# RetNet and RG-LRU decoder layer on one core: the recurrent stage with another gelu, paired exponentials and woven gate tiles

## The chip, the cores and the metric

The kernel runs on one core of one Trainium2 chip. The metric is the device time in microseconds (us), the median of the runs. The core has a matrix engine (TensorE, PE in the profile, with PEld for its weight loads), a vector engine (VectorE, DVE), an activation engine (ScalarE, ACT), a third elementwise engine (GpSimd, POOL) and SyncE (SP), which here only issues transfers.

## The reference, cut to what matters

One decoder layer is computed for 512 prompt tokens and 8 sequences of 4 sample tokens, 544 columns in all, model width 1024. All products are fp32. The part that matters is the recurrent branch, 1536 channels in 12 blocks of 128:

```python
xr, gr = two column blocks of h @ w_in
xconv = causal_conv(xr, conv_buf, conv_w, conv_b)
r = sigmoid(xconv @ w_rg_a + b_rg_a); i = sigmoid(xconv @ w_rg_x + b_rg_x)   # 12 blocks of 128x128
log_a = -8 * r * softplus(-lru_param);  a = exp(log_a)
h_t = a_t * h_(t-1) + sqrt(-expm1(2 * log_a)) * (i * xconv)                  # over time
rnn_y = h * gelu(gr);  branch_rnn = rnn_y @ w_br_rnn
gb = sigmoid(h @ w_mgate + b)        # second half; multiplies branch_rnn
mod = silu(c) @ w_ada + b_ada        # six 1024-wide pieces, for 9 conditioning vectors
```

The retention branch, the mix, the output product and a gated feed-forward network follow.

## The kernel before, in words

Channels lie on the partitions and the 544 tokens on the free axis. A weight slab is 128 x 1024 numbers (512 KB; some are shorter). Each slab is loaded by SyncE, in the one order of the plan. ScalarE then writes its rounded high part (`w_hi`, L982) and VectorE the remainder (`w_lo`, L1276), into rings of three slots. TensorE computes hi*hi, hi*lo and lo*hi for each 128x128 block, each in two halves of 272 columns (`three_passes`, L644), so a tile with eight blocks is 48 matmuls. `split_to(s)` in each engine's program does the splits up to slab s, and `ahead(key)` does them up to two slabs beyond the tile's slab. The high part of slab s can't be written before slab s-3 is multiplied. A product tile lies in one of two PSUM places in turn and must be taken (`took`) before the next but one tile starts.

Every engine has a program written out by hand, and its order sets everything. In the recurrent stage the loop runs over n = 0 to 11. TensorE multiplies the xr tile n, then the small recurrent gates of tile n-1 (`recurrent_gates`, L744, eight fp32 matmuls), then the gr tile n. ScalarE takes xr out of PSUM (four pieces, L1084 to L1088), computes for tile n-1 the two sigmoids, a tanh, an exp and a square root (L1056 to L1062), does the next split, copies gr out of PSUM (L990), and gives the sigmoid of the gelu (L1097), once GpSimd has made its argument. GpSimd makes the gelu from the copy of gr with three products and a final one (L1740 to L1746), and multiplies the input gate with the convolution (`ii`, L1726). VectorE does the convolution (L1353, L1355), the decays (L1364 to L1368), the recurrence with a scan (L1373 to L1383) and the output and its hi and lo parts (L1386, L1284, L1285). `decays` and `recur` of tile n-1 stand at the end of iteration n.

Two loops over eight tiles follow: the gate tiles `gb` (h as the moving side), then the branch tiles `bn` (y as the moving side, 12 blocks in two slabs of 768 columns). Both carry the late part of the modulation: eight chunks of four slabs, each slab four matmuls of 512 columns with the conditioning vectors stationary (`modulation`, L690). One slab stands behind each half tile. Every second tile a finished chunk is copied out by ScalarE (`ada_row`, L1072), turned by TensorE (L700) and added by VectorE (`ada_out`, L1323 and L1324).

Of the kernel before, what the change touches and what calls it, by code (L numbers as in the profile page):

```python
# [24 lines left out]
ALU = mybir.AluOpType  # L25
# [4 lines left out]
P = 128  # L30
# [141 lines left out]
GB_PARTS = (KD // 2, KD // 2)  # L172
# [3 lines left out]
def later_slabs(name, m):  # L176

    first = START_SLABS + 2 * (m + (KD if name == "bn" else 0))
    return first, first + 1


def make_plan():
# [59 lines left out]
    for n in range(NR):  # L242
        pl.whole(("xr", n), 1, [KD])
        if n:
            pl.use_pair(("r", n - 1), 2)
            pl.use_pair(("i", n - 1), 3)
        pl.whole(("gr", n), 1, [KD])
    pl.use_pair(("r", NR - 1), 2)
    pl.use_pair(("i", NR - 1), 3)
    for name, parts in (("gb", GB_PARTS), ("bn", BN_PARTS)):  # L250
        for m in range(KD):
            pl.add_tile((name, m))
            for i, j in enumerate(later_slabs(name, m)):
                pl.add_slab((name, m, "w", i), parts[i] * P)
                pl.step((name, m, "w", i), (name, m))
                chunk_slab(j)
# [33 lines left out]
def slab_source(w, key):  # L290
# [6 lines left out]
    if kind == "gb":  # L297
        return w["w_gb"][key[1], :, key[3] * GB_PARTS[0] * P:(key[3] + 1) * GB_PARTS[0] * P]
# [16 lines left out]
def hybrid_layer_kernel(nc, w, out):  # L315
# [6 lines left out]
    with ExitStack() as top:  # L322
# [51 lines left out]
        gr = sb(rnn, "gr", [P, 2, T])  # L374
        gelu_t = sb(rnn, "gelu_t", [P, T])
        gelu = sb(rnn, "gelu", [P, 2, T])
        rr = sb(rnn, "rr", [P, T])
# [92 lines left out]
        gelu_arg, gelu_sig, gelu_ready, ix_ready = (sem(n) for n in ("gelu_arg", "gelu_sig", "gelu_ready", "ix_ready"))  # L470
# [160 lines left out]
        def _(pe):  # L631
# [115 lines left out]

            for n in range(NR):
# [5 lines left out]
            def turn_later(c):  # L754
                pe.wait_ge(*pair_freed(("ad", c)))
                dst, full = take_pair(("adt", c))
                ada_turn(ada_row[:, c % 2, :], dst[:, 0, :], full)

            recurrent_gates(NR - 1)
            def project_with_modulation(name, m, parts, hi, lo):  # L760


                c = ADA_START + (m + (KD if name == "bn" else 0)) // 2 - 1
                project((name, m), parts, hi, lo, after=[lambda q=q: modulation(q) for q in later_slabs(name, m)],
                        before_last=(lambda: turn_later(c)) if m % 2 == 0 and c >= ADA_START else None)

            for m in range(KD):
                project_with_modulation("gb", m, GB_PARTS, h_hi, h_lo)
            pe.wait_ge(y_ready, NR)
            for m in range(KD):  # L770
                project_with_modulation("bn", m, BN_PARTS, y_hi, y_lo)
# [195 lines left out]
        def _(act):  # L967
# [79 lines left out]
            def gates(n):  # L1047
# [6 lines left out]
                i, u, e, root = (t[:, n % 2, :] for t in (ii, uu, ee, su))  # L1054
                wait_pair(act, ("r", n))
                do(A(halves(rr[:]), ps[:, 4:6, 0:HALF], ACT.Sigmoid, bias=vcol("b_a", n)), *pair_freed(("r", n)))  # L1056
# [3 lines left out]
                do(A(u, rr[:], ACT.Tanh, scale=c4[:, n:n + 1]), u_ready)  # L1060
# [3 lines left out]
            def modulation_rows(name, m):  # L1064

                c, i = divmod(later_slabs(name, m)[1], ADA_PARTS)
                split_to(pl.slab[("ad", c, "w", i)] + AHEAD)
                if i == ADA_PARTS - 1:
                    act.wait_ge(multiplied, pl.tile_end[("ad", c)])
                    if c >= ADA_START + 2:  # L1070
                        wait_pair(act, ("adt", c - 2))
                    do(A(ada_row[:, c % 2, :], ps[0:2 * NSEQ, 4, :], ACT.Copy), *pair_freed(("ad", c)), wait=False)  # L1072

            act.wait_ge(h_ready, KD)
            for n in range(NR):
# [14 lines left out]
                if n:  # L1090
                    gates(n - 1)
                ahead(("gr", n))
                if n >= 2:
                    act.wait_ge(gelu_ready, n - 1)
# [3 lines left out]
            for m in range(KD):  # L1098
                ahead(("gb", m))
                if m == 0:  # L1100
                    gates(NR - 1)
                split_to(pl.slab[("gb", m, "w", 1)] + AHEAD)

                evacuate(("gb", m), gbr[:, m, :], ACT.Sigmoid, bias=vcol("b_gb", m))
                modulation_rows("gb", m)
            for m in range(KD):
                split_to(pl.slab[("bn", m, "w", 1)] + AHEAD)
                modulation_rows("bn", m)
# [155 lines left out]
        def _(dve):  # L1264
# [105 lines left out]
            def recur(n):  # L1370
# [13 lines left out]
                dve.wait_ge(gelu_ready, n + 1)  # L1384

                do(V.tensor_tensor(bb[:], hs[:], gelu[:, n % 2, :], ALU.mult))  # L1386
# [6 lines left out]
            for n in range(NR):  # L1393
# [3 lines left out]
                if n:  # L1397
                    decays(n - 1)
# [518 lines left out]
```

## Time and profile before

| | us |
|---|---|
| median of 3 runs | 1546.73 (1546.11 to 1549.68) |
| span of the profiled execution, first to last instruction | 1542.5 |
| PE busy | 1422.0 (92%) |
| DVE busy | 859.4 (56%) |
| ACT busy | 568.5 (37%) |
| POOL busy | 281.9 (18%) |

The profile gives no other time of its own for the execution than its span; it is 4.2 us under the median of the runs. A busy PE is not PE at its peak, and an engine's share is an average over stages that have different limits, so the stage that the change touches is read by itself.

### The profile page before, as it was taken

To read this page: it belongs to the slowest core of one execution; us is meant where nothing else is said; L and a number is where in the kernel's file an instruction comes from. 1 tells how busy PE (TensorE), PEld (TensorE's weight loads), DVE (VectorE), ACT (ScalarE), POOL (GpSimd) and SP (SyncE) were. 2 spreads that over 40 slices of the span, in tenths; PEclk is the share of its full clock that TensorE was granted. 3 is DMA by queue.
4 is the path that set the end of the run, shared out by engine and by line. 5 is a ranking of instruction groups with operands and counts; after the bars stand their busy time and mean duration, and the time that the engine had idled before them with its cause. 6 is when DMAs were issued, how large, how long until landed. Compare 5 with 4: busy or idle time off the path is not lost.

```text
span 1542.5 us, 24001 instructions
## 1 busy us (share of the span) xinstructions
PE 1422.0 (92%) x10168; PEld 1311.7 (85%) x10168; DVE 859.4 (56%) x1022; ACT 568.5 (37%) x769; POOL 281.9 (18%) x352
## 2 busy tenths in 40 slices
PE   5798887899999999999999999999499999999994
PEld 2498777789999788889879988999399999999993
DVE  4699999844436367537635854773743333332224
ACT  5477666543333332323133232434332222212220
POOL 3364555100012313311320231000200000000002
PEclk9799998999999999999999999999699999999997
DMA  7122112465442524432541443223022222232321
GB/s 319 69 70 68 56 58 86 132 208 169 163 158 94 177 89 148 155 117 85 176 163 62 147 154 123 79 95 145 0 83 92 87 86 93 82 91 76 88 76 58
DMA packets 49499, 172.70 MB, mean 112 GB/s; under 512 B 5488, under 2 KB 5616, under 8 KB 49008
## 3 DMA queue, kind: packets, MB, share of 16 engines
q1 hardware_dynamic: 39024, 135.51, 26.9%
q0 software_dynamic: 9216, 33.56, 6.5%
q10 hardware_dynamic: 1152, 2.10, 0.4%
q8 instruction: 80, 1.31, 0.4%
q14 instruction: 27, 0.22, 0.0%
HBM read 149.82 MB, written 21.32 MB: 111 GB/s over the span
## 4 chain that ended last, share of the span: by engine, by line
PE 64%; DVE 6%; ACT 1%; issue 1%; ACTq 0%; DVEq 0%
PE ps L644 54%; PE ps L853 2%; PE ps L864 2%; PE ps L836 1%; PE ps L880 1%; PE ps L890 1%; PE ps L882 1%; DVE mo L1645 1%; DVE x_res L1646 1%; PE ps L711 1%; DVE s_lo L1458 0%; PE ps L793 0%; DVE rsn L1641 0%; PE ps L806 0%; DVE work L1523 0%
## 5 line engine op out<-in xcount | busy, mean ns | idle before, releaser
L644 PE MATMUL ps<-h_hi,w_hi 128*128 128x272 f32 x2240 | 475.8, 294 | 40.6 <-DVE w_lo L1276 22.3
L644 PE MATMUL ps<-h_hi,w_lo 128*128 128x272 f32 x2240 | 467.6, 291 | 0.0
L644 PE MATMUL ps<-h_lo,w_hi 128*128 128x272 f32 x2240 | 466.2, 290 | 0.0
L644 PEld LDWEIGHTS ps<-h_hi,w_hi 128*128 128x128 f32 x2240 | 359.2, 191 | 51.8 <-issue 39.6
L1276 DVE TENSOR_TENSOR w_lo<-raw,w_hi 128x1024 fp32r<-128x1024 f32 (+3 forms) x204 | 246.4, 1208 | 233.2 <-ACT w_hi L982 229.9
L644 PEld LDWEIGHTS ps<-h_lo,w_hi 128*128 128x128 f32 x2240 | 356.6, 191 | 0.0
L644 PEld LDWEIGHTS ps<-h_hi,w_lo 128*128 128x128 f32 x2240 | 354.0, 191 | 0.0
L982 ACT ACTIVATE w_hi<-raw 128x1024 fp32r<-128x1024 f32 (+3 forms) x204 | 203.0, 995 | 219.8 <-PE ps L644 178.1
L1811 POOL TENSOR_TENSOR mo<-mo,rsn 128x512 f32<-128x512 f32 x6 | 9.6, 1597 | 566.6 <-DVE rsn L1641 566.6
L1558 DVE SCALAR_TENSOR_TENSOR state<-state,ps 128x512 f32<-128x512 f32 x64 | 41.1, 684 | 111.3 <-PE ps L890 111.2
L644 PE MATMUL ps<-a_hi,w_hi 128*128 128x272 f32 x352 | 73.6, 291 | 2.1 <-DVE a_lo L1285 2.1
L644 PE MATMUL ps<-a_hi,w_lo 128*128 128x272 f32 x352 | 73.3, 290 | 0.0
L644 PE MATMUL ps<-a_lo,w_hi 128*128 128x272 f32 x352 | 73.2, 290 | 0.0
L1276 DVE TENSOR_TENSOR w_lo<-ada_late,w_hi 128x1024 fp32r<-128x1024 f32 x32 | 40.2, 1257 | 51.0 <-ACT w_hi L982 50.5
L1145 ACT ACTIVATE s_hi<-state 128x1024 fp32r<-128x1024 f32 x32 | 33.9, 1060 | 81.9 <-PE ps L882 81.9
L1755 POOL DMA_DIRECT2D state<-in_state x32 | 23.4, 731 | 219.5 <-PE ps L700 130.7
L644 PEld LDWEIGHTS ps<-a_hi,w_hi 128*128 128x128 f32 x352 | 56.0, 190 | 2.3 <-DVE a_lo L1285 2.3
L982 ACT ACTIVATE w_hi<-ada_late 128x1024 fp32r<-128x1024 f32 x32 | 33.8, 1057 | 65.3 <-PE ps L644 65.3
L644 PEld LDWEIGHTS ps<-a_lo,w_hi 128*128 128x128 f32 x352 | 56.0, 191 | 0.0
L644 PEld LDWEIGHTS ps<-a_hi,w_lo 128*128 128x128 f32 x352 | 55.5, 191 | 0.0
L690 PE MATMUL ps<-w_hi,c_st 128*18 128x512 f32 x96 | 40.5, 422 | 15.6 <-DVE w_lo L1276 15.5
L644 PE MATMUL ps<-r_hi,w_hi 128*128 128x272 f32 x256 | 53.2, 289 | 1.8 <-DVE acc L1509 1.1
(228 smaller groups left out, 2010.5 us busy)
## 6 DMA issues: line engine op xcount, KB each, us to landing
raw<-in_w_head SPq DMA_DIRECT2D x48, 512.0 KB, 3.6
raw<-in_w_fin SPq DMA_DIRECT2D x44, 512.0 KB, 3.5
ada_late<-in_w_ada SPq DMA_DIRECT2D x32, 512.0 KB, 4.2
state<-in_state POOLq DMA_DIRECT2D x32, 512.0 KB, 4.2
out_rs<-state POOLq DMA_DIRECT2D x32, 512.0 KB, 3.5
raw<-in_w_rnn SPq DMA_DIRECT2D x24, 512.0 KB, 3.7
ada_raw<-in_w_ada SPq DMA_DIRECT2D x16, 512.0 KB, 14.4
raw<-in_w_bret SPq DMA_DIRECT2D x16, 512.0 KB, 3.5
```

What stands on the lines that cost most here:

```text
L644: mm = nc.tensor.matmul(dst[:, half, :], a, b[:, half * HALF:(half + 1) * HALF], start=first and j == 0, stop=last and j == 2)
L690: mm = nc.tensor.matmul(dst[0:2 * NSEQ, :], c_st[:, 2 * i + j, :], part[:, s % RING, j * ADA_CHUNK:(j + 1) * ADA_CHUNK], start=i == 0 and ...
L711: mm = nc.tensor.matmul(ps[:, pl.bank[key][0], 0:HALF], ccol("ones"), src[:, half * HALF:(half + 1) * HALF], start=k == 0, stop=k == n - 1)
L836: mm = nc.tensor.matmul(dst[:, 0:SEQ - j * P], k_r[:, d, j * P:(j + 1) * P], q_r[:, d, j * P:SEQ], start=d == 0, stop=d == 1)
L853: mm = nc.tensor.matmul(dst[:, j * P:SEQ], v_tok[:, j, o * P:(o + 1) * P], scores(j), start=j == 0, stop=j == JT - 1, skip_group_check=True)
L864: mm = nc.tensor.matmul(dst[:, :], k_tok[:, j, d * P:(d + 1) * P], v_tok[:, j, :], start=j == 0, stop=j == JT - 1)
L880: nc.tensor.matmul(ps[0:2 * NS, 7, :], q_st[:, d, at:at + 2 * NS], s_hi[:, e], start=b == 0 and d == 0, stop=False, skip_group_check=True)
L982: A(w_hi[:, i % RING, 0:cols], src[:, 0:cols], ACT.Copy).then_inc(hi_ready, 1)
L1145: do(A(s_hi[:, :], state[:, u % STATES, :, :].rearrange("p d e -> p (d e)"), ACT.Copy), s_hi_ready, wait=False)
L1276: V.tensor_tensor(w_lo[:, i % RING, 0:cols], raw_slab(i)[0][:, 0:cols], w_hi[:, i % RING, 0:cols].bitcast(F32), ALU.subtract).then_inc(lo_ ...
L1558: do(V.scalar_tensor_tensor(state[:, u % STATES, d, :], state[:, u % STATES, d, :], gamma(h) ** TS, ps[:, pl.bank[key][0], :], ALU.mult, A ...
L1755: pool.dma_start(state[:, u % STATES, :, :], w["state"][b, h].rearrange("(d p) e -> p d e", p=P))\
```

## The change

The gelu is one ScalarE instruction with its own function (`Gelu_apprx_tanh`), read straight from PSUM. GpSimd keeps only `ii` and the small copies. Exponentials and roots are no longer made tile by tile: at even n they are made for tiles n-2 and n-1, two exponentials and then two roots (`roots_at`). VectorE's decays and recurrence are done one iteration later, for tile n-2 (`recurrences_at`); iteration 11 does tiles 9 and 10, and tile 11 comes after the first split of the last gate tiles. Gate tiles 0 to 3 are multiplied in iterations 1, 4, 7 and 10, and tiles 4 to 7 in iteration 11 (`GATE_TILES`), each with one slab in place of two half slabs. The modulation is carried by the branch tiles alone: two slabs behind each half tile, so that a branch tile carries a whole chunk.

```diff
-GB_PARTS = (KD // 2, KD // 2)
+GATE_TILES = {1: (0,), 4: (1,), 7: (2,), 10: (3,), NR - 1: (4, 5, 6, 7)}
-def later_slabs(name, m):
+def later_slabs(m, part):
-    first = START_SLABS + 2 * (m + (KD if name == "bn" else 0))
+    first = ADA_PARTS * (ADA_START + m) + 2 * part
     return first, first + 1
+def roots_at(n):
+    if n == NR - 1 or n == NR:
+        return (n - 1,)
+    return (n - 2, n - 1) if n and n % 2 == 0 else ()
+def recurrences_at(n):
+    if n == NR - 1:
+        return (n - 2, n - 1)
+    return (n - 1,) if n == NR else (n - 2,) if n >= 2 else ()
...
# TensorE
                 project(("gr", n), [KD], h_hi, h_lo)
+                if n == NR - 1:
+                    recurrent_gates(n)
+                for m in GATE_TILES.get(n, ()):
+                    project(("gb", m), [KD], h_hi, h_lo)
             for m in range(KD):
+                def modulate(part, m=m):
+                    for q in later_slabs(m, part):
+                        modulation(q)
+                c = ADA_START + m - 1
+                project(("bn", m), BN_PARTS, y_hi, y_lo, y_ready if m == 0 else None, 0,
+                        after=[lambda: modulate(0), lambda: modulate(1)],
+                        before_last=(lambda c=c: turn_later(c)) if m else None)
...
# ScalarE: gates(n) keeps two sigmoids and the tanh
-                do(A(e, rr[:], ACT.Exp, scale=c2n[:, n:n + 1]), e_ready, wait=False)
-                do(A(root, u, ACT.Sqrt), su_ready, wait=False)
+            def roots(tiles):
+                for n in tiles:
+                    do(A(ee[:, n % 2, :], rr[:, n % 2, :], ACT.Exp, scale=c2n[:, n:n + 1]), e_ready, wait=False)
+                for n in tiles:
+                    do(A(su[:, n % 2, :], uu[:, n % 2, :], ACT.Sqrt), su_ready, wait=False)
...
                 if n:
                     gates(n - 1)
+                roots(roots_at(n))
                 ahead(("gr", n))
-                evacuate(("gr", n), gr[:, n % 2, :])
-                act.wait_ge(gelu_arg, n + 1)
-                do(A(gelu_t[:], gelu_t[:], ACT.Sigmoid, scale=GELU_C), gelu_sig, wait=False)
+                if n >= 3:
+                    act.wait_ge(y_ready, n - 2)
+                wait_tile(act, ("gr", n))
+                do(A(halves(gelu[:, n % 3, :]), out_tile(("gr", n)), ACT.Gelu_apprx_tanh), *took(("gr", n)), wait=False)
+                if n == NR - 1:
+                    gates(n)
+                    roots(roots_at(NR))
+                for m in GATE_TILES.get(n, ()):
+                    ahead(("gb", m))
+                    evacuate(("gb", m), gbr[:, m, :], ACT.Sigmoid, bias=vcol("b_gb", m))
...
# VectorE
                 ahead(("xr", n))
                 conv(n)
                 ahead(("gr", n))
-                if n:
-                    decays(n - 1)
-                    recur(n - 1)
+                for i in recurrences_at(n):
+                    decays(i)
+                    recur(i)
+                for m in GATE_TILES.get(n, ()):
+                    ahead(("gb", m))
+                    if n == NR - 1 and m == GATE_TILES[n][0]:
+                        for i in recurrences_at(NR):
+                            decays(i)
+                            recur(i)
             for m in range(KD):
+                split_to(pl.slab[("bn", m, "w", 1)] + AHEAD)
                 wait_took(dve, ("gb", m))
                 wait_tile(dve, ("bn", m))
...
-                if m % 2 == 0:
-                    ada_out(ADA_START + (KD + m) // 2 - 1)
+                if m:
+                    ada_out(ADA_START + m - 1)
...
# GpSimd: the four gelu instructions go
-                do(G.tensor_tensor(gelu_t[:], g, g, ALU.mult))
-                do(G.tensor_scalar(gelu_t[:], gelu_t[:], 0.044715, 1.0, ALU.mult, ALU.add))
-                do(G.tensor_tensor(gelu_t[:], gelu_t[:], g, ALU.mult), gelu_arg)
-                do(G.tensor_tensor(gelu[:, n % 2, :], g, gelu_t[:], ALU.mult), gelu_ready)
```

`rr` and `gelu` get two and three buffers for one and two; `gr` and `gelu_t` go.

## Rows read from the trace of the kernel before

**Rows 1.** Waits by engine: TensorE, 60 to 434 us; total us, times, longest.

```profile
PE ps L644 <- DVE w_lo L1276: 22.3, 13, 3.4
PE ps L744 <- DVE xc L1355: 7.4, 1, 7.4
PE ps L690 <- DVE w_lo L1276: 3.5, 2, 1.8
```

**Rows 2.** Windows: span; busy (instructions) of PE, PEld, DVE, ACT, POOL; clock, DMA.

```profile
78.60:432.40 353.80, 319.83 (x2268) 295.10 (x2268) 271.55 (x337) 201.90 (x268) 112.53 (x119) 0.97 0.34 111
...
184.00:201.50 17.50, 14.46 (x105) 13.57 (x105) 16.91 (x22) 11.60 (x18) 9.44 (x11) 1.00 0.19 61
```

**Rows 3.** Timeline, TensorE: start, us, instruction, idle before and its releaser.

```profile
84.70 2.00 PE L744 MATMUL ps<-xc,rg_w 128*128 128x272 f32 x8
86.33 0.61 PE L644 MATMUL ps<-h_hi,w_hi 128*128 128x272 f32 x2
...
194.90 0.49 PE L644 MATMUL ps<-h_hi,w_hi 128*128 128x272 f32 x2 [2.76 <-DVE w_lo L1276]
```

**Rows 4.** Chain that ended last, in order of time: one tile of eight blocks.

```profile
445.54 6.02 PE ps L644 x48
```

**Rows 5.** Timeline, VectorE, 185 to 201 us: one recurrence, then a convolution.

```profile
185.66 0.43 DVE L1364 TENSOR_SCALAR ee<-ee 128x544 f32<-128x544 f32 x1
...
190.19 1.29 DVE L1383 TENSOR_TENSOR_SCAN hs<-uu,bb 128x544 f32<-128x544 f32 x1
...
193.52 1.23 DVE L1276 TENSOR_TENSOR w_lo<-raw,w_hi 128x1024 fp32r<-128x1024 f32 x1
194.67 1.84 DVE L1353 SCALAR_TENSOR_TENSOR xc<-xp,vec,xc 128x512 f32<-128x512 f32 x1
...
200.03 0.75 DVE L1353 SCALAR_TENSOR_TENSOR xc<-xp,vec,xc 128x512 f32<-128x512 f32 x1
...
200.98 2.26 DVE L1276 TENSOR_TENSOR w_lo<-raw,w_hi 128x1024 fp32r<-128x1024 f32 x1
```

**Rows 6.** Groups by line and shape: GpSimd, 60 to 300 us; busy us, mean ns.

```profile
L1726 POOL TENSOR_TENSOR ii<-ii,xc 128x544 f32<-128x544 f32 x12 | 25.9, 2162 | 0.5 <-ACT uu L1060 0.5
```

**Rows 7.** Timeline, ScalarE, 200 to 210 us: one tile's gates, exponential and root.

```profile
201.49 0.79 ACT L1084 ACTIVATE xc<-ps,vec 128x544 f32<-128x544 f32 x1
...
202.79 0.73 ACT L1056 ACTIVATE rr<-ps,vec 128x544 f32<-128x544 f32 x1
...
206.22 0.75 ACT L1061 ACTIVATE ee<-rr,c2n 128x544 f32<-128x544 f32 x1
206.99 1.28 ACT L1062 ACT_TABLE_LOAD   x1
...
208.85 1.04 ACT L982 ACTIVATE w_hi<-raw 128x1024 fp32r<-128x1024 f32 x1
209.80 0.60 ACT L990 ACTIVATE gr<-ps 128x544 f32<-128x544 f32 x1
```

**Rows 8.** Timeline, a branch tile: TensorE, ScalarE and VectorE.

```profile
386.31 0.39 PE L690 MATMUL ps<-w_hi,c_st 128*18 128x512 f32 x1
...
387.23 0.41 PE L644 MATMUL ps<-y_hi,w_hi 128*128 128x272 f32 x2
...
391.73 0.40 PE L690 MATMUL ps<-w_hi,c_st 128*18 128x512 f32 x1
...
397.25 0.42 PE L700 MATMUL ps<-con,ada_row 18*128 18x18 f32 x4
...
386.57 1.06 ACT L982 ACTIVATE w_hi<-ada_late 128x1024 fp32r<-128x1024 f32 x1 [3.63 <-PE ps L644]
...
388.02 0.83 ACT L982 ACTIVATE w_hi<-raw 128x768 fp32r<-128x768 f32 x1
...
388.88 0.96 DVE L1276 TENSOR_TENSOR w_lo<-raw,w_hi 128x768 fp32r<-128x768 f32 x1
```

**Rows 9.** Transfers, 300 to 434 us: count, KB each, median us to landing.

```profile
ada_late<-in_w_ada SPq DMA_DIRECT2D x23, 512.0 KB, 4.2
```

More of the change, by code:

```diff
@@ L247, in make_plan @@
         pl.whole(("gr", n), 1, [KD])
+        for m in GATE_TILES.get(n, ()):
+            pl.whole(("gb", m), 1, [KD])
     pl.use_pair(("r", NR - 1), 2)
     pl.use_pair(("i", NR - 1), 3)
[L250 to L255, printed above, removed]
+    for m in range(KD):
+        pl.add_tile(("bn", m))
+        for i, n in enumerate(BN_PARTS):
+            pl.add_slab(("bn", m, "w", i), n * P)
+            pl.step(("bn", m, "w", i), ("bn", m))
+            for j in later_slabs(m, i):
                 chunk_slab(j)
@@ L297, in slab_source @@
     if kind == "gb":
[L298 removed]
+        return w["w_gb"][key[1]]
     if kind == "bn":
@@ L373, in hybrid_layer_kernel @@
         xc = sb(rnn, "xc", [P, 2, T])
[L374 to L377, printed above, removed]
+        gelu = sb(rnn, "gelu", [P, 3, T])
+        rr = sb(rnn, "rr", [P, 2, T])
         ii = sb(rnn, "ii", [P, 2, T])
@@ L1059, in gates, with modulation_rows @@
                    wait=False)
-                do(A(u, rr[:], ACT.Tanh, scale=c4[:, n:n + 1]), u_ready)
-                do(A(e, rr[:], ACT.Exp, scale=c2n[:, n:n + 1]), e_ready, wait=False)
-                do(A(root, u, ACT.Sqrt), su_ready, wait=False)
[L1064 to L1072, printed above, removed]
+                do(A(u, rr[:, n % 2, :], ACT.Tanh, scale=c4[:, n:n + 1]), u_ready)
+            def roots(tiles):
[3 more added lines that the diff above has]
+                    do(A(su[:, n % 2, :], uu[:, n % 2, :], ACT.Sqrt), su_ready, wait=False)
+            def modulation_rows(m):
+                c = ADA_START + m
+                split_to(pl.slab[("ad", c, "w", ADA_PARTS - 1)] + AHEAD)
+                act.wait_ge(multiplied, pl.tile_end[("ad", c)])
+                if m >= 2:
+                    wait_pair(act, ("adt", c - 2))
+                do(A(ada_row[:, c % 2, :], ps[0:2 * NSEQ, 4, :], ACT.Copy), *pair_freed(("ad", c)), wait=False)
             act.wait_ge(h_ready, KD)
@@ L1091, in _ @@
                     gates(n - 1)
+                roots(roots_at(n))
                 ahead(("gr", n))
-                if n >= 2:
-                    act.wait_ge(gelu_ready, n - 1)
-                evacuate(("gr", n), gr[:, n % 2, :])
-                act.wait_ge(gelu_arg, n + 1)
-                do(A(gelu_t[:], gelu_t[:], ACT.Sigmoid, scale=GELU_C), gelu_sig, wait=False)
[L1098 to L1105, printed above, removed]
+                if n >= 3:
[8 more added lines that the diff above has]
+                    evacuate(("gb", m), gbr[:, m, :], ACT.Sigmoid, bias=vcol("b_gb", m))
             for m in range(KD):
                 split_to(pl.slab[("bn", m, "w", 1)] + AHEAD)
-                modulation_rows("bn", m)
+                modulation_rows(m)
             def gn_squares(h):
@@ L1711, in _, with inputs, last @@
                 do(G.memset(xp[:, i, 0:3], 0.0))
+            def inputs(n):
+                pool.wait_ge(u_ready, n + 1)
+                do(G.tensor_tensor(ii[:, n % 2, :], ii[:, n % 2, :], xc[:, n % 2, :], ALU.mult), ix_ready, wait=False)
+            def last(n):
+                pool.wait_ge(scanned, n + 1)
+                do(G.tensor_copy(rnn_out[:, n, 0:1], hs[:, SEQ - 1:SEQ]), wait=False)
+                do(G.tensor_copy(rnn_out[:, n, 1:9], samples(hs)[:, :, TS - 1]), last_saved, wait=False)
             for n in range(NR):
```

70 lines of the change are left out of this document (18 added, 52 removed).

## The prediction

> **What bounds the kernel now.** I read the page first: TensorE is busy for 92% of the span and carries most of the chain that ended last, so time is won only where TensorE waits or runs at a low clock. Its busy digits are lowest in the first fifth, outside the load at the start. The list of TensorE's waits from 60 to 434 us [rows 1] shows who is late: VectorE, with the low part of the weights (22.3 + 3.5 us) and once with a convolution (7.4 us). The windows of one iteration [rows 2] show why: of 17.50 us VectorE is busy for 16.91, ScalarE for 11.60. The recurrent stage runs at VectorE's pace. The timeline of VectorE [rows 5] shows that part of this pace is not its own work. The six convolution instructions take 6.31 us (194.67 to 200.98), though the last pair takes 0.95 us, which would be 2.85 for three; a weight split takes 2.26 where another takes 1.23. The long ones lie beside GpSimd's products, and GpSimd is busy for 9.44 us of the tile [rows 2], most of it for the gelu.
>
> **What TensorE needs from 78.6 to 432.4 us**, first to last instruction of the stretch that the change touches. A tile of eight blocks takes 6.02 [rows 4], gates 1.63 (84.70 to 86.33) [rows 3], half a branch tile 4.50 and a modulation slab 0.92 [rows 8], a turn 0.42. So 22 xr and gr tiles 132.4, 12 gates 19.6, 8 gate tiles 48.2, 16 half branch tiles 72.0, 32 slabs 29.4, 8 turns 3.4: 305.0 us. The stretch takes 353.8 [rows 2], so 48.8 is lost: 33.2 in the listed waits [rows 1], about 10.6 to the clock (0.97 granted, 3% of 353.8), the rest in starts after waits. The change leaves TensorE's work as it is. It can give back at most these 48.8, and the question is which new waits stand in their place.
>
> **The change part by part.**
>
> *Gelu.* Four GpSimd instructions, a PSUM copy and a sigmoid of ScalarE become one ScalarE instruction. I price it as the PSUM copy, 0.60 [rows 7]. The trace does not show the function itself, nor whether it shares a table with the sigmoid. Bounds: no load or two loads of 1.28 a tile [rows 7]. I take two, since the exponential and the root each need one of their own here; I count 39 loads of the stage after and 37 now, so ScalarE is not relieved. The load before the gelu runs while ScalarE waits for gr, and it costs TensorE at most 0.3 us in iterations 4 and 10, where xr of the next tile needs gr's PSUM place.
> [...]
>
> *VectorE without the gelu beside it.* A recurrence takes 7.86 (185.66 to 193.52), 5.82 of it to the end of the scan; a split 1.15 start to start; a convolution 2.85 [rows 5]. With two splits that is 13.0 us a tile. What stays beside it is `ii` of 2.16 us [rows 6]. Bounds for what it costs VectorE: nothing, where it falls into idle time, or 2.2 a tile. VectorE lost 3.5 in a convolution and 1.0 in a split to about twice that much GpSimd work, so I take 1.1, in every second tile (in the other it falls where VectorE waits for ScalarE).
>
> *Pairs.* At even n the split of the next gr slab stands behind two exponentials and two roots, and VectorE's own split, and the recurrence behind it, wait for that. The loop is: scan of n-3 ends; ScalarE's gates, pair and split 8.4 (6.06 from 202.79 to 208.85, a second exponential 0.65 and root 0.56, split 1.04, hand-over) [rows 7]; VectorE split 1.15, recurrence 7.86, split 1.15, convolution 2.85, split 1.15, to the end of the next scan but one 5.82; with 1.1 beside GpSimd 29.5 us for two iterations. TensorE needs 27.3 for two iterations and 33.4 with a gate tile in them. So VectorE falls 2.2 behind in the two pairs without a gate tile and catches up in the others. Iteration 4, counted from the end of its xr tile: scan of tile 1 at 3.6, ScalarE to 12.0, VectorE's split 13.2, recurrence 21.0, low part of gr 5 at 22.2, while TensorE arrives at 1.63 + 3 x 6.02 + 1.63 = 21.3. So about 1.0 us is lost in each of iterations 4, 7 and 10, with the PSUM place 3.5 in all.
>
> *Iteration 11.* Counted from the end of xr 11: ScalarE takes it out in 1.3, then 6.06 and a split [rows 7], VectorE has the split of gate tile 5 at 9.6. Behind it stand two recurrences (15.7, with 1.1 beside GpSimd), then the split of gate tile 6, at 27.5. TensorE arrives at 1.63 + 6.02 + 1.63 + 12.04 = 21.3 and waits 6.2. Then the recurrence of tile 11 stands before the split of gate tile 7: 36.5, TensorE at 33.5, 3.0 more. The clock after such a wait: 1.6 us, an estimate, a sixth of the 10.6 lost now in six slow spells. The 7.4 us wait for the convolution goes: conv 11 is done 8 us before its gates.
>
> *Modulation behind the branch tiles.* Two slabs in place of one after each half tile. The ring of three then ties the next raw slab to the half tile just multiplied: ScalarE starts 0.26 after it, VectorE 0.86 later, 0.96 for the split, 0.14 to TensorE (194.75 to 194.90 in [rows 3, 5]): 2.22, against 1.84 of two modulation slabs [rows 8]. That is 0.38 lost in the middle of each of eight tiles, and about 0.25 at the end of seven, where VectorE also takes the tile and adds the turned chunk: 4.9 us. In exchange the half-width gate slabs go.
>
> *Buffers.* The third gelu buffer and the second `rr` are free of waits in this order. SyncE's list has the modulation slabs later and the gate slabs earlier, in the plan's order; at the start the slabs come as now.
>
> **The sum.** New losses 3.5 + 9.2 + 1.6 + 4.9 = 19.2, in place of 48.8: 29.6 less. The span goes from 1542.5 to 1512.9. The median of the runs lies 4.2 above the span now, so 1517 us.
>
> **The rivals.**
>
> (a) *TensorE never waits in the recurrent stage.* If VectorE runs ahead more than I work out, the 3.5 and most of the 9.2 go, and the time is 1505 (1498.6 were there no new wait at all). For it: the gate tiles bring 48 us of TensorE work with only 9 of VectorE's. Against: the three recurrences in a row in iteration 11 are in the program's order.
>
> (b) *The loop through both engines is longer.* If `ii` costs VectorE 2.3 in every tile and ScalarE's chain grows by 1 to 2 us, the loop is about 33 us a pair against 27.3 and 33.4: 5 lost in two pairs, 1 to 2 in three, 2 more at the end, 12 in all: 1529. For it: `ii` alone takes 2.16 now, and VectorE's own splits double beside GpSimd. [...]
>
> (c) *Slower: the branch tiles starve.* A branch tile brings four slabs of 512 KB and two of 384 KB in 13.1 us. The last modulation slab is asked for 3.9 us after the tile before ends, lands 4.2 later [rows 9] and is first needed 8.6 after it was asked for. To eat the whole gain each of eight tiles must lose 3.7 us, so the landing must take over 12.3 us. A landing of 14 us would lose 5.4 a tile, 43 in all, and give 1560. Against it: the transfers of the stretch are far from that.
>
> (d) *The change does nothing*, since something else sets the pace. TensorE's waits name VectorE each time, so this is hardly left.
>
> **How the numbers follow.** Forecast 0.68, (a) 0.12, (b) 0.14, (c) 0.04, (d) 0.02. The forecast's own range is 1510 to 1525 (each of 3.5, 9.2 and 4.9 from half to one and a half of itself). The range over the cases is 1506 to 1532. A change within 0.3% (4.6 us) can't be told from none in this kernel. Faster by more: 0.94; within: 0.03; slower: 0.03.
>
> **What would show it.** In the profile after: no `gelu_t`; splits of raw slabs near 1.23 and convolution pairs near 0.95 except beside `ii`; TensorE's waits for w_lo of some 6 and 3 us before gate tiles 6 and 7 and nowhere else above 1.5; the wait for xc gone; waits of 0.4 us before half the raw slabs of the branch tiles. The forecast is wrong if iterations 2 to 10 still take over 15 us without a gate tile, if the branch tiles take over 14.5 us each, or if the gelu instruction takes much more than 0.6.

## The result and the profile after

| | before | after |
|---|---|---|
| median of the four executions, us | 1548.02 | 1519.76 |
| median without the one at a low clock, us | 1548.02 | 1519.44 |
| span of the profiled execution, us | 1542.5 | 1517.3 |
| last turn of the late modulation, us from the start | 432.45 | 404.25 |

One of the four executions of the changed kernel ran at a granted clock of 0.556 throughout and took 2353.28 us; the ratio, 0.9815 with an interval of 0.9801 to 0.9829, and every comparison below go by the other three, 1519.44. The forecast was 1517.0, so it was 2.4 us too low (2.8 against the median of all four), and the gain is 28.6 us.

First the line of busy times of the changed kernel (busy us, share of the span, instructions).

```profile
PE 1421.0 (94%) x10168; PEld 1305.5 (86%) x10168; DVE 818.3 (54%) x1014; ACT 565.6 (37%) x751; POOL 221.8 (15%) x304
```

TensorE's work is the same (1421.0 us busy, 1422.0 before). GpSimd lost 60 us of work, and VectorE lost 41 us with only eight instructions fewer (1014 against 1022, half slabs joined).

TensorE's waits from 60 to 440 us, which answer to [rows 1]: total us, times, longest.

```profile
PE ps L658 <- DVE w_lo L1293: 11.0, 5, 5.9
```

The 13 waits for `w_lo` of [rows 1] are five, the two before modulation slabs are gone, and so is the one for `xc`. The timeline of TensorE shows where the five are, with two turns (L714) and the last one. The first of the five, 3.42 us, ends where the stretch begins; before has 2.92 us there, ended by ScalarE.

```profile
77.83 0.79 PE L658 MATMUL ps<-h_hi,w_hi 128*128 128x272 f32 x2 [3.42 <-DVE w_lo L1293]
...
156.24 0.49 PE L658 MATMUL ps<-h_hi,w_hi 128*128 128x272 f32 x2 [0.22 <-DVE w_lo L1293]
...
278.13 0.79 PE L658 MATMUL ps<-h_hi,w_hi 128*128 128x272 f32 x2 [5.94 <-DVE w_lo L1293]
...
287.13 0.49 PE L658 MATMUL ps<-h_hi,w_hi 128*128 128x272 f32 x2 [1.16 <-DVE w_lo L1293]
...
306.70 0.49 PE L658 MATMUL ps<-y_hi,w_hi 128*128 128x272 f32 x2 [0.23 <-DVE w_lo L1293]
...
318.16 0.42 PE L714 MATMUL ps<-con,ada_row 18*128 18x18 f32 x4
...
331.99 0.42 PE L714 MATMUL ps<-con,ada_row 18*128 18x18 f32 x4
...
404.25 0.42 PE L714 MATMUL ps<-con,ada_row 18*128 18x18 f32 x4 [0.76 <-ACT ada_row L1091]
```

The recurrent gates (L758) start 13.87 us after the last ones, or 19.88 where a gate tile is woven in, but for three iterations that take 0.14 to 0.45 more; before it was mostly 17.5 [rows 2]. The turns (L714) stand 13.83 apart, one for each branch tile. From the start after the first wait to the last turn it is 326.4 us, against 353.8 [rows 2].

The windows of the stretch and of two iterations, with the columns of [rows 2]:

```profile
77.80:404.30 326.50, 317.10 (x2269) 289.35 (x2269) 230.39 (x329) 199.17 (x250) 50.42 (x71) 0.98 0.37 121
...
202.20:230.20 28.00, 28.00 (x210) 27.06 (x209) 23.99 (x36) 21.07 (x29) 7.39 (x9) 1.00 0.28 92
```

In the second row TensorE is busy for all 28.00 us: the recurrent stage now runs at TensorE's pace. VectorE still has 4 us of room in it.

The groups by line and shape, 60 to 412 us (busy us, mean ns, idle before):

```profile
L1293 DVE TENSOR_TENSOR w_lo<-raw,w_hi 128x1024 fp32r<-128x1024 f32 x32 | 39.1, 1230 | 36.8 <-ACT w_hi L996 36.1
...
L1370 DVE SCALAR_TENSOR_TENSOR xc<-xp,vec,xc 128x512 f32<-128x512 f32 x36 | 34.7, 964 | 9.1 <-ACT xs L1107 8.3
L1372 DVE SCALAR_TENSOR_TENSOR xc<-xs,vec,xc 128x32 f32<-128x32 f32 x36 | 12.2, 338 | 0.0
...
L1726 POOL TENSOR_TENSOR ii<-ii,xc 128x544 f32<-128x544 f32 x12 | 21.6, 1802 | 6.0 <-ACT uu L1075 5.7
...
L1116 ACT ACT_TABLE_LOAD x12 | 15.4, 1283 | 5.8 <-PE ps L658 5.6
...
L1116 ACT ACTIVATE gelu<-ps 128x544 f32<-128x544 f32 x12 | 7.5, 625 | 0.7 <-PE ps L658 0.6
```

The same view of before, 60 to 440 us:

```profile
L1353 DVE SCALAR_TENSOR_TENSOR xc<-xp,vec,xc 128x512 f32<-128x512 f32 x36 | 44.1, 1225 | 1.1 <-POOL xs L1716 0.2
L1276 DVE TENSOR_TENSOR w_lo<-raw,w_hi 128x1024 fp32r<-128x1024 f32 x25 | 39.8, 1592 | 16.5 <-ACT w_hi L982 15.8
L1355 DVE SCALAR_TENSOR_TENSOR xc<-xs,vec,xc 128x32 f32<-128x32 f32 x36 | 29.6, 821 | 0.0
```

`ii` took 2162 ns [rows 6]. So the same instructions became shorter on both engines: a split by 0.36 us, a wide convolution instruction by 0.26, a narrow one by 0.48, `ii` by 0.36. The gelu takes 0.625 us and one table load per tile; with the loads of the other functions there are 39 in the stage, as counted ahead.

### The profile page after: what moved, and what is told of

Read it like the earlier page. It is cut to its first block, busy times and chain, and to the rows that moved or that the text cites. A ratio compares the mean times of both kernels' runs of the same rounds, so it can differ in the third digit from the quotient of the medians.

```text
span 1517.3 us, 23874 instructions
## 1 busy us (share of the span) xinstructions
PE 1421.0 (94%) x10168; PEld 1305.5 (86%) x10168; DVE 818.3 (54%) x1014; ACT 565.6 (37%) x751; POOL 221.8 (15%) x304
## 4 chain that ended last, share of the span: by engine, by line
PE 65%; DVE 6%; ACT 1%; issue 1%; ACTq 0%; DVEq 0%
PE ps L658 55%; PE ps L867 2%; PE ps L878 2%; PE ps L850 1%; PE ps L894 1%; PE ps L904 1%; PE ps L896 1%; DVE mo L1655 1%; DVE x_res L1656 1%; DVE s_lo L1468 0%; PE ps L725 0%; PE ps L807 0%; DVE rsn L1651 0%; PE ps L820 0%; DVE work L1533 0%
## 5 line engine op out<-in xcount | busy, mean ns | idle before, releaser
L1293 DVE TENSOR_TENSOR w_lo<-raw,w_hi 128x1024 fp32r<-128x1024 f32 (+2 forms) x196 | 236.2, 1207 | 277.6 <-ACT w_hi L996 274.0
L996 ACT ACTIVATE w_hi<-raw 128x1024 fp32r<-128x1024 f32 (+2 forms) x196 | 202.0, 1031 | 284.4 <-PE ps L658 229.3
L1683 DVE TENSOR_TENSOR a_tmp<-a_tmp,ps 128x544 f32<-128x544 f32 x22 | 15.9, 721 | 70.3 <-PE ps L658 70.3
L658 PE MATMUL ps<-r_lo,w_hi 128*128 128x272 f32 x256 | 52.9, 288 | 0.0
L658 PE MATMUL ps<-r_hi,w_lo 128*128 128x272 f32 x256 | 52.8, 287 | 0.0
```

The lines of the kernel that those rows point to most:

```text
L658: mm = nc.tensor.matmul(dst[:, half, :], a, b[:, half * HALF:(half + 1) * HALF], start=first and j == 0, stop=last and j == 2)
L996: A(w_hi[:, i % RING, 0:cols], src[:, 0:cols], ACT.Copy).then_inc(hi_ready, 1)
L1293: V.tensor_tensor(w_lo[:, i % RING, 0:cols], raw_slab(i)[0][:, 0:cols], w_hi[:, i % RING, 0:cols].bitcast(F32), ALU.subtract).then_inc(lo_ ...
L1683: do(V.tensor_tensor(halves(t), halves(t), out_tile(("fu", n)), ALU.mult), *took(("fu", n)))
```

## The experiments

Each was timed beside the kernel before, whose median was 1547.66 to 1547.96 in these sessions, within 0.4 us of the 1548.02 above. "The whole change" is the changed kernel with its 1519.44. The first four ask which part of the change carries the time.

**The gelu alone.** The kernel before, with the gelu in ScalarE and two `rr` buffers; order, pairs and modulation as before.

```diff
                 if n >= 2:
-                    act.wait_ge(gelu_ready, n - 1)
-                evacuate(("gr", n), gr[:, n % 2, :])
-                act.wait_ge(gelu_arg, n + 1)
-                do(A(gelu_t[:], gelu_t[:], ACT.Sigmoid, scale=GELU_C), gelu_sig, wait=False)
+                    act.wait_ge(y_ready, n - 1)
+                wait_tile(act, ("gr", n))
+                do(A(halves(gelu[:, n % 2, :]), out_tile(("gr", n)), ACT.Gelu_apprx_tanh), *took(("gr", n)), wait=False)
...
# GpSimd: its four gelu instructions go
```

> The kernel before with one part of the change: the gelu by one ScalarE instruction from PSUM, GpSimd's four gelu instructions gone (rr gets a second buffer so that nothing races). No pairs, no woven gate tiles, modulation as before. Theory G (the gelu beside VectorE and the wait of ScalarE for it were the loss): VectorE needs 13.0 us a tile and 1.1 beside ii, 14.1, TensorE 13.9; so iterations 1 to 11 take 14.1 to 14.5 us instead of 17.5, the 7.4 us wait for the convolution goes, and the time is 1512 to 1520, about that of the whole change. Rival W (the woven gate tiles are what gives VectorE room): with two more table loads a tile in ScalarE's chain and no gate tiles between, iterations stay near 16 us and the time is 1530 or more.

Measured: 1511.15 us (1509.85 to 1512.02), ratio 0.9764 (0.9745 to 0.9784). That is 0.9 us under the range that was expected. The gelu alone gives more than the whole change, by 8.3 us. TensorE's waits, 60 to 440 us, and the one inside the stretch that is over 3 us (the 4.1 for `xs` ends where the stretch begins):

```profile
PE ps L642 <- ACT xs L1086: 4.1, 1, 4.1
PE ps L742 <- DVE xc L1352: 3.2, 1, 3.2
PE ps L688 <- DVE w_lo L1273: 2.0, 2, 1.7
...
PE ps L642 <- DVE w_lo L1273: 0.3, 1, 0.3
```

```profile
236.58 3.99 PE L742 MATMUL ps<-xc,rg_w 128*128 128x272 f32 x8 [3.21 <-DVE xc L1352]
```

Most iterations take 13.87 us with exponentials and roots still tile by tile, and the last three 14.10, 14.12 and 14.37, so 1.0 us in all was left for pairs to win. The last turn is at 397.41.

**The whole change without it.** The changed kernel, with the gelu given back to GpSimd as before.

```diff
-                wait_tile(act, ("gr", n))
-                do(A(halves(gelu[:, n % 3, :]), out_tile(("gr", n)), ACT.Gelu_apprx_tanh), *took(("gr", n)), wait=False)
+                evacuate(("gr", n), gr[:, n % 3, :])
+                act.wait_ge(gelu_arg, n + 1)
+                do(A(gelu_t[:], gelu_t[:], ACT.Sigmoid, scale=GELU_C), gelu_sig, wait=False)
...
# GpSimd: the four gelu instructions are back
```

> The changed kernel with the gelu by GpSimd again (copy of gr in three buffers, the final product in place), all else as changed: pairs, woven gate tiles, late modulation. Theory G: VectorE is slowed as before (17.5 us a tile), which the four woven gate tiles hide only in part: iterations 1 to 11 take about 192 us instead of 176.5, so 1535 to 1542. Rival W: the order is what gained, and the time stays under 1526.

Measured: 1545.29 (1543.91 to 1547.4), ratio 0.9987 (0.9978 to 0.9997): what the order wins by itself is under the 0.3% that can be told. Here it fell outside what was expected, on the slow side. TensorE's waits:

```profile
PE ps L659 <- DVE w_lo L1295: 25.0, 13, 7.2
```

The order does not take the pressure from VectorE: 25.0 us in 13 waits stand against 22.3 in 13 of [rows 1]. It removes the wait of 7.4 us for `xc`, and brings one of 7.2 us before gate tile 6, whose split stands behind two recurrences in a row.

**No pairs.** The changed kernel, exponential and root tile by tile.

```diff
 def roots_at(n):
-    if n == NR - 1 or n == NR:
-        return (n - 1,)
-    return (n - 2, n - 1) if n and n % 2 == 0 else ()
+    return (n - 1,) if n else ()
```

> The changed kernel with exponential and root of one tile in each iteration (two loads a tile instead of two a pair), recurrences where the change has them. If ScalarE has room (theory of the prediction: it is not relieved by the pairs and not the bound), within 3 us of the changed kernel, 1517 to 1523. Rival: the pairs shorten the loop that sets VectorE's pace, and without them 5 us or more are lost, 1525 or more.

Measured: 1516.17 (1513.07 to 1518.67), ratio 0.9791 (0.9765 to 0.9816). The interval overlaps that of the whole change, and the median is 0.8 us under the range that was expected. The saved table loads win nothing: ScalarE is not what TensorE waits for. In the profiles the ten iterations from gates 0 to gates 10 take 162.7 us without pairs and 163.5 with them, so the pairs cost 0.8.

**Another order of iteration 11.** The recurrences of tiles 9, 10 and 11 no longer stand in a row: behind the first VectorE does the splits of gate tiles 6 and 7, behind the second those of the first branch slab and the first modulation slab, and ScalarE does one split ahead of its last gates and one ahead of its last root.

```diff
# ScalarE: its two splits are moved too
...
# VectorE, behind ahead(("gr", n)); the old place of tile 11's recurrence goes
+                if n == NR - 1:
+                    tiles = GATE_TILES[n]
+                    for i, ms in ((n - 2, tiles[:2]), (n - 1, tiles[2:]), (n, ())):
+                        decays(i)
+                        recur(i)
+                        for m in ms:
+                            ahead(("gb", m))
+                    continue
```

> The changed kernel with iteration 11 in another order: VectorE does the recurrence of tile 9, the splits of gate tiles 6 and 7, the recurrence of tile 10, the splits of the first branch slab and the first modulation slab, then the recurrence of tile 11; ScalarE does those splits before gates and roots of tile 11. Theory: the waits of 5.9 and 1.2 us before gate tiles 6 and 7 and the slow clock behind them (3 us) go: 9 to 10 us faster than the changed kernel, about 1510. Rival: the three recurrences only move their delay to the first branch tiles, which then wait for weights or y, and the time stays within 3 us of the changed kernel.

Measured: 1509.54 (1508.9 to 1512.93), ratio 0.9759 (0.9738 to 0.9781), 9.9 us under the whole change, as expected. The waits of 5.94 and 1.16 us are gone. What TensorE still waits for VectorE's weights from 60 to 440 us:

```profile
PE ps L704 <- DVE w_lo L1299: 0.6, 1, 0.6
PE ps L658 <- DVE w_lo L1299: 0.5, 2, 0.3
```

The next two ask why the gelu was dear. Nobody needed GpSimd's results early, so was it the wait for them, or their running beside VectorE?

**GpSimd's work, with nobody waiting for it.** The gelu-only kernel, and four GpSimd instructions of the same kinds and shapes as the old gelu, whose result nothing reads.

```diff
# beside the edit of the gelu alone; gelu_t is filled once
+                do(G.tensor_tensor(gelu_u[:], gelu_t[:], gelu_t[:], ALU.mult))
+                do(G.tensor_scalar(gelu_u[:], gelu_u[:], 0.044715, 1.0, ALU.mult, ALU.add))
+                do(G.tensor_tensor(gelu_u[:], gelu_u[:], gelu_t[:], ALU.mult))
+                do(G.tensor_tensor(gelu_u[:], gelu_t[:], gelu_u[:], ALU.mult))
```

> The kernel of the first run (before with the gelu by ScalarE) and on GpSimd four instructions as long as the four gelu ones, on numbers that nobody uses and nobody waits for. It tells apart the two ways in which the gelu on GpSimd could hold VectorE back. Theory C (VectorE's instructions are stretched beside GpSimd's): the whole gain goes again, iterations near 17.5 us, 1538 to 1548. Theory S (ScalarE waited for the gelu's argument, 54 us in all, and gave its weight splits late): the gain stays, 1511 to 1518.

Measured: 1552.58 (1549.12 to 1553.97), ratio 1.0026 (1.0016 to 1.0035). The whole gain is gone; the time lies 4.6 us over the range that was expected. The same nine iterations, from gates 1 to gates 10, first here and then in the gelu-only kernel, with the columns of [rows 2]:

```profile
99.28:256.28 157.00, 137.37 (x939) 132.71 (x937) 151.46 (x187) 113.78 (x144) 93.18 (x93) 0.92 0.19 60
```

```profile
99.49:225.37 125.88, 125.59 (x938) 122.14 (x937) 120.35 (x187) 112.86 (x144) 39.26 (x54) 1.00 0.24 75
```

VectorE's same 187 instructions are busy for 31.1 us more, and the nine iterations take 31.1 us more; VectorE's idle time is 5.5 us in both. The timelines of VectorE and of GpSimd around one convolution:

```profile
196.81 1.84 DVE L1352 SCALAR_TENSOR_TENSOR xc<-xp,vec,xc 128x512 f32<-128x512 f32 x1
198.57 1.07 DVE L1354 SCALAR_TENSOR_TENSOR xc<-xs,vec,xc 128x32 f32<-128x32 f32 x1
199.68 1.19 DVE L1352 SCALAR_TENSOR_TENSOR xc<-xp,vec,xc 128x512 f32<-128x512 f32 x1
200.79 1.34 DVE L1354 SCALAR_TENSOR_TENSOR xc<-xs,vec,xc 128x32 f32<-128x32 f32 x1
202.17 1.90 DVE L1352 SCALAR_TENSOR_TENSOR xc<-xp,vec,xc 128x512 f32<-128x512 f32 x1
204.00 0.24 DVE L1354 SCALAR_TENSOR_TENSOR xc<-xs,vec,xc 128x32 f32<-128x32 f32 x1
```

```profile
195.77 2.33 POOL L1725 TENSOR_TENSOR ii<-ii,xc 128x544 f32<-128x544 f32 x1
198.06 1.54 POOL L1738 TENSOR_TENSOR gelu_u<-gelu_t 128x544 f32<-128x544 f32 x1
199.69 0.65 POOL L1739 TENSOR_SCALAR gelu_u<-gelu_u 128x544 f32<-128x544 f32 x1
200.42 1.67 POOL L1740 TENSOR_TENSOR gelu_u<-gelu_u,gelu_t 128x544 f32<-128x544 f32 x1
202.16 1.36 POOL L1741 TENSOR_TENSOR gelu_u<-gelu_t,gelu_u 128x544 f32<-128x544 f32 x1
```

Six instructions take 7.46 us from 196.81 to the start of the next at 204.27, against 2.85 for the same work free of GpSimd (three times the last pair of [rows 5], as in the forecast). None of them was idle before its start. The first five run while GpSimd runs; the last, which starts at 204.00 after GpSimd's last has ended at 203.52, takes 0.24. That settles it: the cost is the running beside each other, not the wait for the gelu.

The rows also show what kind of cost it is. The narrow instructions, of 0.24 us when alone, end 0.04 us after the GpSimd instruction beside them has ended (199.64 after 199.60, 202.13 after 202.09). The wide ones, of 0.75 when alone, end 0.53 to 0.55 after it (198.65 after 198.10, 200.87 after 200.34, 204.07 after 203.52). That is not the picture of two engines that share a speed. It is that of a VectorE instruction held back until the running GpSimd instruction ends. This is read from five rows; no run tests it by itself, and the spans of GpSimd are rough.

**One more product of GpSimd where VectorE has room.** The changed kernel, with a second product like `ii` ahead of `ii` in tiles 0 to 9.

```diff
+                if n < NR - 2:
+                    do(G.tensor_tensor(y_lo[:, NR - 1, :], ii[:, n % 2, :], xc[:, n % 2, :], ALU.mult))
                 do(G.tensor_tensor(ii[:, n % 2, :], ii[:, n % 2, :], xc[:, n % 2, :], ALU.mult), ix_ready, wait=False)
```

> The changed kernel with one more GpSimd product of 128x544 before the input product of tiles 0 to 9 (its result is overwritten unused). The prediction's price for such a product is 1.1 us of VectorE where VectorE is busy, and VectorE has about 4 us of room in 28 in the changed kernel: 0 to 4 us slower, 1520 to 1524. If a product costs VectorE its own length (rival b of the prediction), 5 us or more slower.

Measured: 1519.07 (1518.24 to 1522.08), ratio 0.9818 (0.9802 to 0.9835), no change against the whole change that the timing can tell. TensorE got four waits between 0.25 and 0.92 us. The profiles tell more: from gates 0 to gates 10 it is 165.8 us here and 163.5 in the changed kernel (163.6 in its variant with two late buffers, the last run below). The ten products thus cost 2.3 us, 0.23 each, which the total hides, since the untouched rest after the last turn was 2.4 us shorter in this profile (1110.6 against 1113.0). VectorE's room of some 4 us in a pair of iterations takes up most of such running beside, not all: 0.23 us a product, where the four instructions of the run above, with VectorE as the bound, cost 3.5 us a tile.

The last four look at what the order of the change still costs.

**The reordered iteration 11 without pairs.** The two edits above together.

> The changed kernel with the tail order of the fourth run and without pairs as in the third. If the two add, the 9 us of the first and the 3 us of the second: about 1507. If the 3 us of the third run came from the clock and not from the missing pairs, 1509 to 1511.

Measured: 1508.33 (1506.25 to 1509.81), ratio 0.9741 (0.9723 to 0.9759). It has the lowest median of all, under both kernels, and lies between the two values that were expected (1507, and 1509 to 1511). Its interval overlaps those of the gelu alone and of the reordered iteration 11, so it is not told apart from them.

**The gelu alone, with the last gates later.** The wait of 3.21 us for `xc` in the gelu-only kernel, attacked: recurrent gates 11 stand behind the first half of gate tile 0.

```diff
-            recurrent_gates(NR - 1)
...
-                project((name, m), parts, hi, lo, after=[lambda q=q: modulation(q) for q in later_slabs(name, m)],
+                after = [lambda q=q: modulation(q) for q in later_slabs(name, m)]
+                if (name, m) == ("gb", 0):
+                    first = after[0]
+                    after[0] = lambda: (recurrent_gates(NR - 1), first())
+                project((name, m), parts, hi, lo, after=after,
```

> The kernel of the first run with TensorE's recurrent gates of tile 11 moved behind the first half of gate tile 0, so that the 3.2 us wait for the convolution of tile 11 is covered by work. Expected: 1506 to 1509, 2 to 5 us faster than the first run. Rival: the wait goes to the second half of gate tile 0, whose weights VectorE splits only after the decays of tile 10: no faster than 1510.

Measured: 1516.16 (1514.13 to 1516.97), ratio 0.9794 (0.9779 to 0.9809), 5.0 us slower than the gelu alone where 2 to 5 us faster was expected. The rival that was named with it came in: the wait goes to the second half of gate tile 0. The timeline shows it:

```profile
239.10 0.40 PE L688 MATMUL ps<-w_hi,c_st 128*18 128x512 f32 x1 [1.35 <-ACT rr L1057]
...
247.52 0.61 PE L688 MATMUL ps<-w_hi,c_st 128*18 128x512 f32 x1 [4.25 <-DVE w_lo L1276]
```

TensorE no longer waits for `xc`, and comes so much earlier to the slab that stands next: there it waits for ScalarE's gates to free PSUM, and then for a split that VectorE does only behind convolution 11 and recurrence 10. The 3.21 turned into 5.6 before two slabs. In the profiles, whose spans differ by 3.2 us, the stretch is 2.0 longer (321.3 against 319.4), and the rest after the last turn, which the edit doesn't touch, 2.2.

**No weaving.** The changed kernel, with all eight gate tiles in iteration 11.

```diff
-GATE_TILES = {1: (0,), 4: (1,), 7: (2,), 10: (3,), NR - 1: (4, 5, 6, 7)}
+GATE_TILES = {NR - 1: tuple(range(KD))}
```

> The changed kernel with all eight gate tiles behind iteration 11, none woven in (one line). Theory: in the loop of pairs VectorE needs 29.5 us for two iterations and TensorE 27.7, and no gate tile lets it catch up; 1.5 us lost in each of four to five pairs, the tail as in the changed kernel: 5 to 8 us slower than it, 1524 to 1528. Rival (from the third and sixth run, where there was more room than worked out): VectorE keeps up anyway, within 3 us of the changed kernel.

Measured: 1528.79 (1527.82 to 1531.14), ratio 0.9876 (0.986 to 0.9893), 9.4 us slower than the whole change, a little more than the 5 to 8 that were expected. TensorE's waits:

```profile
PE ps L658 <- DVE w_lo L1293: 12.1, 7, 3.5
PE ps L758 <- DVE xc L1372: 5.0, 1, 5.0
```

There are waits of 1.29, 1.25 and 1.26 us in iterations 6, 8 and 10 (at 151.04, 180.50 and 209.97), the even ones, in which the pairs are made, and the wait for the last convolution is back with 4.98. The woven tiles buy these off. The pairs seem to be what needs them: the gelu-only kernel, without pairs and without woven tiles, has one wait of 0.28 for `w_lo` in its iterations. That is argued and not shown, since that kernel also does its recurrences one iteration earlier, and no run has the changed kernel with neither pairs nor woven tiles.

**Two buffers for late modulation.** The changed kernel, `ADA_RING` 2 for 3.

> The changed kernel with two buffers instead of three for the late modulation slabs, so that each of their transfers is asked for about one modulation slab and half a branch slab later. It tests the room that the prediction gave the transfers of the branch tiles (4 us between landing and first need). If the room is there: 0 to 4 us slower than the changed kernel. If the transfers are near the bound (rival c): 2 us and more in each branch tile, 1535 and more.

Measured: 1519.65 (1517.37 to 1521.38), ratio 0.9813 (0.9799 to 0.9828), no change. The transfers of the branch tiles have more room than they need. Its profile has a first wait of 3.5 us, waits of 5.93 and 1.16 before gate tiles 6 and 7, and turns 13.8 apart, like that of the whole change.

## Why the prediction was right, step by step

**The cause of the gain held.** With GpSimd's four instructions gone, a raw split takes 1.23 us as priced, a convolution pair 1.30 in the mean and the 0.95 of the price where `ii` doesn't run beside it, and iterations without a gate tile take 13.87 us. The two gelu experiments show that this step carries the whole gain (36.7 us alone, 2.6 us for all the rest without it), and the one with work that nobody waits for shows its mechanism.

**The sum's terms.** The forecast had 19.2 us of new losses in place of 48.8, a gain of 29.6 in the stretch. Measured are 353.8 - 326.4 = 27.4. The total is nearly right in part because a term that was too large (3.5 us for 0.9) and terms that were left out (2.2 and 2.6) offset each other:

- 3.5 us in iterations 4, 7 and 10 was too much. The starts of the gates stand 0.45, 0.15 and 0.25 us further apart in three iterations, 0.9 in all: VectorE was less late than the loop of 29.5 us a pair said. The wait before gr 5 that was worked out is there (156.24), with 0.22 us for about 0.9; behind the woven tiles of iterations 7 and 10 TensorE has no listed wait. The run without pairs has none of the 0.9.
- The 6.2 us before gate tile 6 was 5.94. The timeline of VectorE has the split where the order put it, behind two recurrences:

```profile
260.02 0.43 DVE L1381 TENSOR_SCALAR ee<-ee 128x544 f32<-128x544 f32 x1
...
267.88 0.44 DVE L1381 TENSOR_SCALAR ee<-ee 128x544 f32<-128x544 f32 x1
...
274.98 1.74 DVE L1302 TENSOR_TENSOR y_lo<-bb,y_hi 128x544 fp32r<-128x544 f32 x1
276.76 1.23 DVE L1293 TENSOR_TENSOR w_lo<-raw,w_hi 128x1024 fp32r<-128x1024 f32 x1
```

- The 3.0 us before gate tile 7 was 1.16, and the clock is why. The granted clock after the 5.94 us wait was 0.52 for 3.7 us, about the level of 1.2 GHz, and TensorE arrived later at gate tile 7:

```profile
278.10:281.80 3.70, 3.67 (x16) 3.70 (x17) 3.53 (x6) 0.39 (x1) 0.00 (x0) 0.52 0.74 237
```

  Half of 3.7 us, 1.8, is the clock's price, near the 1.6 forecast (a sixth of 10.6 is in fact 1.8). At the full clock gate tile 6, started at 278.13, would have ended at 284.15 and the wait up to 287.13 would have been the 3.0 that was worked out. The forecast counted the clock and the 3.0 one after the other, where the one hid in the other. Together 9.2 + 1.6 became 5.94 + 1.16 + 1.8 = 8.9.
- The branch tiles take 13.83 us for 13.10 of work (two halves of 4.50, four slabs of 0.92 and a turn of 0.42): 0.73 lost in each, 5.1 in the first seven, where 4.9 was forecast for all (the forecast's own terms add up to 4.8). The timelines show the chain that was worked out: the half tile ends, ScalarE starts 0.26 later, VectorE 0.87 after that, TensorE 1.02 after that. Less the 1.84 of two slabs that is 0.31 in the middle of a tile, where 0.38 was worked out, and so leaves 0.42 at its end for 0.25. The wait stands in the row of TensorE's weight load (PEld), 0.66 us for `w_lo`; the matmul rows list none there.

```profile
338.94 0.40 PE L704 MATMUL ps<-w_hi,c_st 128*18 128x512 f32 x1
...
341.09 0.30 PEld L658 LDWEIGHTS ps<-y_hi,w_hi 128*128 128x128 f32 x2 [0.66 <-DVE w_lo L1293]
341.09 0.52 PE L658 MATMUL ps<-y_hi,w_hi 128*128 128x272 f32 x2
```

```profile
339.20 0.85 ACT L996 ACTIVATE w_hi<-raw 128x768 fp32r<-128x768 f32 x1 [3.19 <-PE ps L658]
```

```profile
340.07 0.96 DVE L1293 TENSOR_TENSOR w_lo<-raw,w_hi 128x768 fp32r<-128x768 f32 x1 [2.81 <-ACT w_hi L996]
```

- Left out was 0.2 us in each of eleven iterations, 2.2 in all: by single prices two tiles and gates are 13.67, and TensorE takes 13.87 though it is busy throughout.
- Left out was also the clock in the first tile: from 77.83 to the gates at 86.54 it is 8.71 us, against 6.10 in [rows 3], at a granted clock of 0.66 against 1.00. 2.6 us, behind the wait of 3.42 (before 2.92). The length of the wait doesn't say what follows: in the gelu-only kernel a wait of 4.07 is followed by 7.60 us at 0.78.

These terms are 0.9 + 8.9 + 5.1 + 2.2 + 2.6 = 19.7 of the 21.4 us by which the stretch is over the 305.0 that TensorE needs; 1.7 stays unassigned (the last branch tile is in it).

The forecast did not look past the last turn. The rest of the program, which the change does not touch, took 1110.05 us in the profile of before and 1113.05 in that of the changed kernel. TensorE waits the same there. Both kernels have the same wait of 2.3 us for `s_lo`, and the 10 us after it read, first after, then before:

```profile
513.50:523.50 10.00, 9.94 (x32) 6.35 (x33) 4.99 (x8) 1.54 (x2) 2.15 (x4) 0.51 0.26 97
```

```profile
541.70:551.70 10.00, 9.91 (x63) 7.83 (x64) 5.03 (x8) 1.88 (x3) 2.39 (x5) 1.00 0.44 132
```

TensorE started 32 matmul records in one and 63 in the other: the granted clock fell to 0.51 in one and stayed in the other. It is not the change that makes it fall. In the same 10 us the granted clock is 0.51 to 0.66 in the profiles of all ten experiments too, those with the four GpSimd instructions per tile left in included; of twelve profiles that of before is the only one with 1.00. What decides it is open, as it is for the first tile, and it isn't all of the difference: the run with two `ii` has 0.66 there and 1110.6 us after the last turn.

**The offset of 4.2 us.** It was taken as the time around the span. In the timed executions that list both, time less span is 1.8 to 3.6 us, mostly about 2, and 2.1 in the changed kernel's profiled one (1519.44 less 1517.3). So the execution of before that was profiled took some 1544.6 us (an estimate, from 1542.5 and that 2.1), about 2 less than the median that the forecast used and 3.4 less than 1548.02. About half of the 4.2 us was thus the profile of a quick execution, and it made up, without intent, for part of the longer rest. The span was forecast at 1512.9 and measured 1517.3: 2.2 of these 4.4 us lie in the stretch, 3.0 behind it, and 0.8 were gained ahead of it. With 2.1 us around the span the forecast would have been 1515.0, and 4.4 too low. That it was only 2.4 too low is luck.

**Slips in the recorded working** that change little. With no new wait at all it would be 1497.9 us and not 1498.6 (1546.73 less 48.8). Half to one and a half of the three terms gives 1508 to 1526 and not 1510 to 1525. The lowest busy digit of TensorE inside the span is not in its first fifth but a 4 at about 1100 us, past the stretch.

**The signs that were named.** Iterations, branch tiles and the gelu lie within their limits (13.87 of 15, 13.83 of 14.5, 0.625 for 0.6), and the wait for `xc` is gone. Of the waits of 6 and 3 us the second was 1.16, and the 3.42 at the start of the stretch was not foreseen.

**The rivals.** (a), no waits in the recurrent stage: its mechanism did not come about in the changed kernel, but reordering iteration 11 made most of it (1509.54, with 1505 worked out). For iterations 1 to 10 it is nearly right, with 0.9 us lost. (b), a longer loop: out, the loop takes TensorE's time and no more. The Trainium skill (ScalarE: Activation LUTs, What ACT_TABLE_LOAD costs) puts a switch of tables at about 2.66 us, of which 1.28 are the load. The trace agrees on the load (1.283 us in the mean) and not on the rest: the gelu starts 1.30 us after its load begins (258.79 the load, 260.09 the gelu). (c), transfers: out, a buffer less changes nothing. (d): out.

**What the forecast did not ask** is what each part gives alone. Against the gelu alone the order of the change costs 8.3 us. The profiled spans differ by 8.2: 7.0 in the stretch (326.4 against 319.4, from the start after the first wait to the last turn), 1.4 in the rest, less 0.2 ahead of it. In the stretch the branch tiles lose 5.1, where those of the gelu-only kernel with one slab behind each half tile lose nothing: between two turns TensorE is busy in all of

```profile
340.05:362.20 22.15, 22.15 (x165) 20.13 (x165) 10.19 (x12) 7.77 (x9) 0.00 (x0) 1.00 0.51 169
```

with 22.10 of work by the same prices. The waits are 7.6 against 5.5 us. As far as these runs show, the weaving repays what the pairs cost, and neither is needed once GpSimd is quiet. A weight ring of four slots, which would loosen the tie between a half tile and the next raw slab, wasn't tried; nor was the late modulation moved by itself, so its 5.1 us are read from the timelines and from no run of their own.

## What to carry to other kernels

Where VectorE sets the pace, look at the same instruction's durations: if they differ by a factor of two, see what GpSimd does at those times, and take that work off before any order is changed. Try the parts of a large change alone: here one of them gave all of the gain and the rest took 8.3 us of it back. Several long pieces in a row on the engine that also prepares the next operands make a wait that can be counted ahead; putting those operands' work between the pieces removes it.

## What was not expected of the hardware

- Work beside GpSimd stretched VectorE far more than by its share: an instruction of 32 columns took 1.07 and 1.34 us where it takes 0.24, and ended 0.04 us behind the GpSimd instruction beside it. Four GpSimd instructions of 5.2 us in all (1.54, 0.65, 1.67, 1.36) cost each iteration 3.5 us (157.00 less 125.88 over nine). In the whole kernel that is 41 us, though nobody waited for their result.
- The low clock (0.51 to 0.66) behind the 2.3 us wait for `s_lo` is in eleven of twelve profiles, whatever the kernel, and not in that of before. The time after the last turn is 1110.6 to 1114.3 us in the ten experiments, 1113.05 after and 1110.05 before. Up to 4 us of a span thus come from work that no edit touches, so a difference of that size between two profiles is to be looked for in the stretch itself.
